# One layer of a pooling and short-conv decoder: the second norm of tiles 8-15 turned by DMA, conv and pooling work moved between engines, own buffers for the first tiles, a new order

## The reference, cut to what matters

```python
def trunk_layer(x, c, pool_buf, conv_buf, ffn_buf, pos0, ...):
    mod = (jax.nn.silu(c) @ w_ada + b_ada)[:, None, :]
    sh1, sc1, gt1, sh2, sc2, gt2 = jnp.split(mod, 6, axis=-1)
    h = rmsnorm(x, g_pre_mix) * (1 + sc1) + sh1
    proj = h @ w_in                                        # 1024 -> 2048
    v_pool, x_conv, gate_b, gate_c = jnp.split(proj, ...)  # 512 each
    y_pool = pool_mixer(...)     # window mean (2/4/8/16) - v, 128x128 map per group
    conv_in = jnp.concatenate([conv_buf, gate_c * x_conv], axis=1)
    y_conv = gate_b * causal_dwconv(conv_in, conv_w)       # 3 taps
    mix = jnp.concatenate([y_pool, y_conv], axis=-1) @ w_out
    x = x + gt1 * rmsnorm(mix, g_post_mix)
    h2 = rmsnorm(x, g_pre_ffn) * (1 + sc2) + sh2
    up = h2 @ ffn_w_up                                     # 1024 -> 5632
    a, b = jnp.split(causal_dwconv(ffn_in, ffn_conv_w), 2, axis=-1)   # ffn_in: carried rows, up
    f = (jax.nn.silu(a) * b) @ ffn_w_down                  # 2816 -> 1024
    x = x + gt2 * rmsnorm(f, g_post_ffn)
```

## Time and profile before

| | us |
|---|---|
| median of 3 runs (lowest, highest) | 727.0 (725.28, 727.85) |
| the profiled execution | 726.18 |
| its span on the slowest core (core 2) | 724.6 |
| spans of the 8 cores | 718.5 to 724.6 |
| TensorE busy | 694.0 (96%) |
| VectorE / ScalarE / GpSimd busy | 468.5 / 311.1 / 267.5 |
| granted TensorE clock, mean of core 2 | 0.989 |

### The profile page before, as it was taken

One profiled execution on the slowest core, in us unless ns is written; L12 is line 12 of the kernel. 1 busy time (PEld: TensorE's weight loads), 2 busy tenths in 40 slices (PEclk: granted clock), 3 DMA queues, 4 the chain that ended last, 5 costly groups with the idle time before them and its releaser, 6 DMA issues.

```text
span 724.6 us, 12059 instructions; the slowest of 8 cores (718.5 to 724.6 us)
## 1 busy us (share of the span) xinstructions
PE 694.0 (96%) x4049; PEld 331.3 (46%) x4049; DVE 468.5 (65%) x636; ACT 311.1 (43%) x554; POOL 267.5 (37%) x274
## 2 busy tenths in 40 slices
PE   5889989999989999999999999999999999999996
PEld 2445535444445544444444444444444444444442
DVE  2659699754659998777777411138777777758403
ACT  5255544334657764444544211144454544433111
POOL 1102255333858634424444132214333333223220
PEclk8999999999999999999999999999999999999999
DMA  8999877996999667556899964113335433061422
GB/s 249 161 240 181 194 124 131 156 192 169 178 277 275 221 116 124 97 127 100 147 156 155 221 222 137 58 59 59 59 66 95 74 59 59 1 228 68 144 105 72
DMA packets 23532, 100.71 MB, mean 139 GB/s; under 512 B 3184, under 2 KB 3696, under 8 KB 18608
## 3 DMA queue, kind: packets, MB, share of 16 engines
q0 software_dynamic: 9072, 47.71, 39.9%
q1 hardware_dynamic: 14400, 52.23, 22.6%
HBM read 127.02 MB, written 20.63 MB: 204 GB/s over the span
## 4 chain that ended last, share of the span: by engine, by line
PE 73%; DMA 14%; issue 4%; DVE 4%; POOL 2%; ACT 2%; DVEq 0%; SPq 0%; POOLq 0%; ACTq 0%
PE ps L520 72%; DMA big<-x 5%; DMA scp<-w_scp 3%; DMA y<-big 2%; POOL big L559 2%; DMA wsh<-w_sh 1%; DMA ring<-w_inc 1%; PE ps L530 1%; DVE big L555 1%; POOL by L559 1%; DVE ta L555 1%; DVE ss L559 0%; DVE q L555 0%; PE ps L538 0%; ACT xc L551 0%
## 5 line engine op out<-in xcount | busy, mean ns | idle before, releaser
L520 PE MATMUL ps<-ah,ring 128*128 128x512 bf16 (+2 forms) x2240 | 407.2, 342 | 4.4 <-DVE q L555 2.0
L520 PEld LDWEIGHTS ps<-ah,ring 128*128 128x128 bf16 x2240 | 187.8, 98 | 212.8 <-issue 6.6
L555 DVE SCALAR_TENSOR_TENSOR big<-ps,misc,big 128x1022 f32<-128x1022 f32 (+1 forms) x176 | 224.5, 1281 | 69.5 <-ACT halob L551 32.5
L559 POOL TENSOR_TENSOR g<-big 128x1024 bf16<-128x1024 f32 x44 | 104.5, 2375 | 171.6 <-DVE big L559 91.0
L551 ACT ACTIVATE big<-ps,misc 128x1024 f32<-128x1024 f32 x88 | 97.9, 1113 | 140.1 <-PE ps L520 139.9
L520 PE MATMUL ps<-wdn,g 128*128 128x512 bf16 x704 | 153.1, 379 | 0.0
L559 POOL TENSOR_TENSOR big<-big 128x256 f32<-128x256 f32 (+2 forms) x51 | 65.1, 1279 | 121.0 <-DVE big L555 94.1
L520 PEld LDWEIGHTS ps<-wdn,g 128*128 128x128 bf16 x704 | 68.5, 98 | 82.1 <-issue 0.4
L551 ACT ACTIVATE big<-ps 128x1024 bf16<-128x1024 f32 (+2 forms) x30 | 28.9, 964 | 123.4 <-PE ps L520 116.2
L666 DVE RECIPROCAL stat<-stat 128x1 f32<-128x1 f32 (+1 forms) x64 | 9.7, 157 | 106.3 <-ACT stat L551 105.6
L520 PE MATMUL ps<-wo,by 128*128 128x512 bf16 x256 | 58.2, 384 | 0.0
(11 more groups left out here) (130 smaller groups left out, 464.1 us busy)
## 6 DMA issues: line engine op xcount, KB each, us to landing
ring<-w_up POOLq DMA_DIRECT2D x22, 1024.0 KB, 9.9
y<-big SPq DMA_DIRECT2D x27, 512.0 KB, 3.2
big<-y SPq DMA_DIRECT2D x16, 512.0 KB, 3.8
big<-x SPq DMA_DIRECT2D x7, 1024.0 KB, 8.9
big<-x SPq DMA_DIRECT2D x12, 512.0 KB, 9.2
wdn<-w_down POOLq DMA_DIRECT2D x11, 512.0 KB, 12.8
wg<-w_gate POOLq DMA_DIRECT2D x4, 1024.0 KB, 11.1
scp<-w_scp POOLq DMA_DIRECT2D x8, 384.0 KB, 6.9
```

What stands on the lines that cost most here:

```text
L520: inst = e.matmul(bank_ap, l, r, start=(first and i == 0), stop=(last and i == len(pairs) - 1))
L555: return K.op(eng, lambda e: e.scalar_tensor_tensor(out, in0, s, in1, op0, op1), reads=reads, writes=writes, cost=c_dve(n))
L559: return K.op(eng, lambda e: e.tensor_tensor(out, in0, in1, op), reads=reads, writes=writes, cost=c_dve(n) if eng == "dve" else c_pool(n))
```

## The change

1. Second norm: tiles 0-15 are kept in eight buffers `xnp`. Tiles 0-7 are still turned by TensorE; tiles 8-15 by DMA transposes from `xnp` into `ah`, issued on SP during the first up projection (`turn_by_dma`), each followed per four tiles by the modulation. `xnp` lies over the modulation weights `w2` 0-3.
2. Third conv term: ScalarE scales it into `xc`, GpSimd adds it to `ta`; the product with b goes from GpSimd to VectorE.
3. Start: tiles 0-7 have seven `xn` buffers instead of three, and the squares are written to `junk` instead of `xn`. The square-root table of ScalarE is loaded before x arrives.
4. Smaller moves: the samples' window sums from VectorE to GpSimd, scaling of the pool map and the pool state's bias from VectorE to ScalarE; w_out waits for fewer regions.
5. A new `PROJ` order and three planner costs. `UPAT` is -1 three times, so the first `w_up` loads wait for the gate row as before.

```diff
 PROJ = """
-T:0 T:1 T:2 T:3 T:4 T:5 T:6 T:7 a:0 s:0,0 s:0,1 a:1 s:1,0 s:1,1 a:2 s:2,0 s:2,1 a:3 s:3,0 s:3,1 a:4 s:4,0 s:4,1
+T:0 T:4 T:1 a:0 T:2 T:3 T:6 a:1 a:2 s:0,0 T:7 T:5 s:1,0 s:0,1 s:2,0 s:1,1 a:3 s:3,0 s:2,1 s:3,1 a:4 a:5 a:6
...
+FIRST_T = 8
+UPAT = (-1, -1, -1)
...
-    RATE = 330e3
+    RATE = 315e3
...
+    XNP = [alloc("xnp", [128, D], BF16, at=cur[0] + 2048 * i) for i in range(8)]
...
+    XN += [alloc("xn", [128, D], BF16, at=cur[0] + 2048 * i) for i in range(4)]
...
+    JUNK = [alloc("junk", [128, D], BF16), alloc("junk", [128, D], BF16, at=ta_at)]
...
-        return (0.16 if mode > 1.0 or n < 256 else 0.21) + n / 960.0 / mode
+        return (0.19 if n < 256 else 0.16 if mode > 1.0 else 0.21) + n / 960.0 / mode
...
-        return 0.15 + n * 2.2 / 1000.0
+        return 0.15 + n * (2.2 if n < 512 else 2.7) / 1000.0
...
+    K.op("act", lambda e: e.activation(out=STAT[:, 7, 19:20], in_=EPSB, func=AF.Sqrt), reads=[r_sc, r_eps], cost=0.3)
...
+        if k == ST2 and t < 16:
+            N, r_n = XNP[t % 8], r_xnp[t % 8]
+        else:
+            j = t % (NXN + 4) if t < 8 else t % NXN
+            N, r_n = XN[j], r_xn[j]
...
+        if k == ST1:
+            h = t % 2 if t < 8 else 0
+            stats(X[0:rows, :], rows, k, t, [r_x], JUNK[h][0:rows, :], [r_junk[h]])
...
+    def turn_by_dma(t):
+
+        K.dma("sp", lambda e: [e.dma_start_transpose(out=AH[:, :, t * 128:t * 128 + 128], in_=XNP[t - 8])], s_xnp[t - 8], 1,
+              reads=[r_xnp[t - 8]], writes=[r_ah[kc][t] for kc in range(KC)], deps=[up_op[-1]], nbytes=524288, row=2048)
+        if t % 4 == 3:
+            modulate(list(range(t - 3, t + 1)), G2T, S2T, r_m2)
...
-            ts(POOLW[:, g, :], PWF[:, g, :], VECS[:, V_PSC + g:V_PSC + g + 1], None, ALU.mult, None, [r_pwf, r_vecs], [r_poolw], 128)
+            act(POOLW[:, g, :], PWF[:, g, :], AF.Copy, [r_pwf, r_vecs], [r_poolw], 128, scale=VECS[:, V_PSC + g:V_PSC + g + 1])
...
-                tt(dst[:, lo:W], src[:, lo:W], src[:, lo - sh:W - sh], ALU.add, [r_src], [r_dst], W - lo)
+                tt(dst[:, lo:W], src[:, lo:W], src[:, lo - sh:W - sh], ALU.add, [r_src], [r_dst], W - lo, eng="pool")
...
-        for m, w in ((1, w1), (0, w0)):
-            stt(sh(TA[k]), v[m], w, sh(TA[k]), ALU.mult, ALU.add, [rq, r_ta[k], r_vecs], [r_ta[k]], n)
+        act(sh(XC[k]), v[0], AF.Copy, [rq, r_vecs], [r_xc[k]], n, scale=w0)
+        tt(TA[k][:, 0:n], TA[k][:, 0:n], XC[k][:, 0:n], ALU.add, [r_ta[k], r_xc[k]], [r_ta[k]], n, eng="pool")
+        stt(sh(TA[k]), v[1], w1, sh(TA[k]), ALU.mult, ALU.add, [rq, r_ta[k], r_vecs], [r_ta[k]], n)
         if c < 4:
-            tt(BY[:, 4 + j, c0:c0 + n], TA[k], TB[k], ALU.mult, [r_ta[k], r_tb[k]], [r_by[4 + j][c]], n, eng="pool")
+            tt(BY[:, 4 + j, c0:c0 + n], TA[k], TB[k], ALU.mult, [r_ta[k], r_tb[k]], [r_by[4 + j][c]], n)
...
-                r.alias(pool_regs)
+                r.alias(r_v[0] + r_v[1] if hb == 0 else r_v[1][1:] + r_v[2] + r_v[3])
...
-            if t < 16:
+            if t < FIRST_T:
                 turn_tile(t, o_xn[t], "act" if t % 2 else "dve")
...
+            if gi == 0 and FIRST_T <= i + 6 < 16:
+                turn_by_dma(i + 6)
```

More of the change, by code:

```diff
@@ L677, in stats2 @@
              writes=[r_stat[k + 1][16]], cost=0.16)
-    r_xn = [R() for _ in range(NXN)]
-    xn_i = [0]
+    r_xn = [R() for _ in range(NXN + 4)]
+    r_junk = [R() for _ in range(2)]
     r_ah = [[R() for _ in range(17)] for _ in range(KC)]
@@ L697, in norm_tile @@
-        return j
-    def turn_tile(t, j, eng, bank=None):
+        if k == ST2 and t < 16:
[3 more added lines that the diff above has]
+            N, r_n = XN[j], r_xn[j]
+        if t == 16 and k == ST2:
+            stats2(X[:, 0:512], k, [r_x], N[:, 0:512], [r_n])
+            ts(N[:, 0:512], X[:, 0:512], STAT[:, k + 1, 16:17], None, ALU.mult, None, [r_x, r_stat[k + 1][t]],
+               [r_n], 512, mode=2.0)
+            return N, r_n
@@ new lines, in norm_tile @@
+        if k == ST1:
+            h = t % 2 if t < 8 else 0
+            stats(X[0:rows, :], rows, k, t, [r_x], JUNK[h][0:rows, :], [r_junk[h]])
+        else:
+            stats(X[0:rows, :], rows, k, t, [r_x], N[0:rows, :], [r_n])
+        ts(N[0:rows, :], X[0:rows, :], STAT[0:rows, k + 1, t:t + 1], None, ALU.mult, None,
+           [r_x, r_stat[k + 1][t]], [r_n], D, mode=2.0)
+        return N, r_n
+    r_xnp = [R() for _ in range(8)]
+    s_xnp = [new_sem("xnp%d" % i) for i in range(8)]
+    def turn_by_dma(t):
[3 more added lines that the diff above has]
+            modulate(list(range(t - 3, t + 1)), G2T, S2T, r_m2)
@@ L701, in turn_tile @@
+    def turn_tile(t, xn, eng, bank=None):
         r0, rows = tile_rows(t)
+        N, r_n = xn
         b = take() if bank is None else bank
         psb = PSF[:, b, :].bitcast(BF16).rearrange("p (k n) -> p k n", k=KC)
-        o = tr([psb[:, kc, 0:rows] for kc in range(KC)], [XN[j][0:rows, kc * 128:(kc + 1) * 128] for kc in range(KC)],
-           IDB[0:rows, 0:rows], [r_xn[j], r_idb], [r_bank[b]], 0.5)
+        o = tr([psb[:, kc, 0:rows] for kc in range(KC)], [N[0:rows, kc * 128:(kc + 1) * 128] for kc in range(KC)],
+           IDB[0:rows, 0:rows], [r_n, r_idb], [r_bank[b]], 0.5)
@@ L819, in tile_in @@
         turn_tile(t, p1a[t], TURNS[t], (turn_b + [None])[t % (5 - START)] if t < 8 else None)
+        if t == 7:
+            r_ta[0].alias(r_junk[1:])
+            for i in range(4):
+                r_s[i].alias(r_xn[NXN + i:NXN + i + 1])
     def start_step(kc, c):
@@ L1049, in ada2 @@
         if kc < 4:
-            r_usb.alias([r_w2[kc]])
+            for r in r_xnp:
+                r.alias([r_w2[kc]])
         elif kc < 6:
@@ L1186, in up_load @@
     def up_load(gi, pb):
-        up_slot[gi, pb] = ring_load(wup_d[pb], KC * 512, deps=gate_in if gi == 0 and pb < 3 else ())
+        up_slot[gi, pb] = ring_load(wup_d[pb], KC * 512, deps=() if gi or pb > 2 else [o_ops[UPAT[pb]]] if UPAT[pb] >= 0 else gate_in)
     r_yd = [R() for _ in range(17)]
@@ L1247, in o_mm @@
         for hb in range(2):
-            mm(PSF[0:rows, b + hb, :], [(BY[:, kc, r0:r0 + rows], WO[hb][:, kc, :]) for kc in range(KC)],
+            o_ops[t] = mm(PSF[0:rows, b + hb, :], [(BY[:, kc, r0:r0 + rows], WO[hb][:, kc, :]) for kc in range(KC)],
                [r_by[kc][c] for kc in range(KC)] + r_wo[hb], [r_bank[b + hb]], 512)
-    o_xn = {}
+    o_xn, o_ops = {}, {}
     singles[:] = [6, 7]
@@ L1348, in up_group @@
                     tmps[:] = [4, 5]
+            if gi == 0 and FIRST_T <= i + 6 < 16:
+                turn_by_dma(i + 6)
+            if gi == 0 and i == 10:
+                r_usb.alias(r_xnp)
             pb = i // 2
```

36 lines of the change are left out of this document (14 added, 22 removed).

## The result

The changed kernel takes 761.8 us (750.4 to 769.7, 4 runs) against 726.7 (725.3 to 727.9) for the kernel before in the same runs: ratio 1.041, interval 1.036 to 1.046. It is 4% slower; I had forecast 717.0.

A forecast was written before the change was run, and what follows sets the result against it. The prediction took TensorE's own work plus its losses before 300 us to bound the kernel. Gains of 3.6+0+2.9+3.5 = 10.0 us took the 727.0 us median to 717.0, range 712.5 to 724.5.

The forecast's parts named there:

- The DMA transposes: First up projection: eight 256 KB DMA transposes on SP, costed at nothing, covered by DMA room at share 0.65.
- Rival 1: Up projection: DMA transposes take the engines and TensorE waits; 734 us at 9.9 us each; chance 0.04.
- What stands behind them: Up projection: transposes' result first read by second up group, 16 modulations fit VectorE's slack; costed at nothing.
- Turns, 3.6 us: Output projection: eight fewer turns of tiles 8-15 on TensorE, 0.45 us each, 3.6 us gained.
- the other three terms: Start, projections' conv units and output projection's x stall: gains of 0, 2.9 and 3.5 us.
- Conv units, 2.9 us: Projections: work moved off VectorE recovers part of 7.5 us of TensorE idle and slow clock; 2.9 us gained.
- The x stall, 3.5 us: Output projection: earlier gate row and w_up loads shrink the wait for x; 3.5 us gained, bounds 0 and 4.7.
- Start, 0: Start: earlier gains are waited for again at 82.83 us; 0 us, ends 0.7 slower and 1 faster.
- The sum: Whole kernel: gains of 3.6, 0, 2.9 and 3.5 us make 10.0, for a median of 717.0 us.

The follow-up runs named there:

- plain_copy_in_up: Changed kernel with each DMA transpose replaced by a plain DMA copy of the same 256 KB, same places and queue; ratio to before 0.992.
- transposes_in_down: Changed kernel with all eight DMA transposes and their modulations moved to the first down projection; ratio to before 0.992, 0.991 when run again.
- before_and_down_turns: Kernel before with one part alone: tiles 8-15 kept in xnp and turned by DMA transposes during the first down projection; ratio 0.998.
- down_old_order_chain: transposes_in_down with both the order of steps and the conv chain of the kernel before; ratio to before 0.992.
- no_up_loads: Changed kernel with modulations held until later pairs and the w_up loads after the first three left out; ratio to before 0.994.
- modulate_late: Changed kernel with modulations of tiles 8-15 placed later in the code, at the nineteenth and twenty-first pair; ratio to before 1.052.
- modulate_held: Changed kernel with modulations of tiles 8-15 made to wait for matmuls of the eighteenth and twentieth pair; ratio to before 1.050, 766.3 us.

## Why the prediction was wrong

*The DMA transposes* are the step that failed: "I cost all of it at nothing; its cover is the DMA room". I bounded the price by a plain store, 2.1 us, and a w_up load, 9.9, and gave the outcome in which they take the engines 0.04. Alone a transpose takes 3.0 us, near the end that I took. But the price is not a property of the transfer: beside the weight loads it is 6 to 14 us on a lucky core of the changed kernel, up to 46 to 59 on the others, and the load's own goes from 9 to 45. Rival 1 had the right sign and the right place. It asked for an average of 7.8 us over all eight, and core 5 has 22.8; but it took this for a fixed price of one transfer, and what decided was the chance that a core collapses, 23 of 32 spans here, where one of eight is enough. Taken from plain_copy_in_up, which keeps all but the transposing (0.992 against 1.041), the step costs some 35 us. The cover that I named (share 0.65) was cover for bytes; and I counted the transposes' own bytes, not what they do to the packets of others.

*What stands behind them.* I said that the result is first read by the second up group, and put the 16 modulations on VectorE's slack. They stood in its in-order queue, and VectorE waited 19.3 us. That was an error too, but not the cause: held back, they save nothing.

*Turns, 3.6 us:* the mechanism was right, the size is not shown. Four of the eight lie behind the last w_out matmul, and from before to transposes_in_down that stretch goes from 160.5 to 158.7 us, 1.8 for four. But alone in the kernel before (before_and_down_turns) the same step gained 1.2 us in all (0.998), and the stretch grew to 161.8: TensorE sits idle there for 3.7 us on the mean of the cores, where before has 1.4, so new waits took what the turns gave. In the changed kernel the step is worth more than 3.6: 1.001 with the turns on TensorE, 0.992 with the eight in the down projection, on one chip, some 6 us. With the turns on TensorE the stretch is 165.4: TensorE waits for the second norm (up to 2.47 us before one turn; idle 4.5 us on the mean). What in the rest of the change brings these waits was not tried. So the other three terms, 6.4 us in my sum, gave nothing as long as TensorE did the turns (1.001).

*Conv units, 2.9 us:* wrong. The output projection does not start earlier, 172.9 us on the mean of the changed kernel and 173.9 and 174.7 in the two runs with the turns in the down projection, against 172.7; TensorE waits for q as before. Its idle time between 75 us and that start is 5.8 us on the mean of the cores and was 6.0; I had forecast 3 to 5. I moved 9.3 us off VectorE and took some of TensorE's 7.5 for it, without showing that those waits are VectorE's load and not the length of the chain from q, which the edit did not shorten.

*The x stall, 3.5 us:* the mechanism was right, gate row, w_up, y store and x in turn, with 1.7 us of wait left of 6.5 on core 2. The gate row's store is issued at 131.1 on core 5, where it was at 140.0 on core 2 of the kernel before, and takes 23.8 us where it took 26.5. The size was that of one core: core 2 and core 1 of the kernel before have the stall (65.4 and 66.3 us in the stage), cores 0 and 5 do not (60.3 and 61.0). The mean goes from 62.9 to 60.7 and 59.4; if the turns are 1.8 of it, 0.4 to 1.7 us are left for this term.

*Start, 0:* the second tile is turned at 82.7 as forecast, and the output projection starts no earlier. But before_and_down_turns (0.998) and down_old_order_chain (0.992) differ only in the start, the smaller moves, the buffers of the second norm and the planner's costs, 0.7% or 5 us, mostly in the output projection (60.8 to 59.0) and behind it (161.8 to 160.0). Which of them it is was not separated and stays open; so does how much of it is the chip.

*The sum:* with the transposing out of the way the kernel gains 5.7 us (721.35 against 727.09), not 10.0.

## What to carry to other kernels

Look at all cores before the page of the slowest: a cost that hits a core by chance is paid almost always when the time is the maximum of eight. Do not price a new kind of transfer from one of its size: ask what runs beside it, and try it at a quiet place first, since here a move of the same eight DMAs by some 130 us turned 4% slower into 0.8% faster. Try a part alone and also leave it out of the whole: the same turns were worth 1.2 us one way and some 6 the other. A term read from the slowest core's trace needs a look at the others: a stall that two or three of eight have is worth less than it shows.

## What the runs showed of the hardware

A DMA transpose of 128x1024 bf16 from SBUF to SBUF lands in 3.0 to 3.2 us alone, on eight cores at once, and its issue takes 1.22 us on SP (no_up_loads). Beside the 1 MB w_up loads, which cast to bf16 on GpSimd's queue, there are two outcomes. Either transposes and loads take up to some 16 us each (cores 1, 3 and 6 of the changed kernel: transposes up to 14.1, loads 8 to 17). Or both stall each other: transposes take up to 59.4 us and loads 38 to 47 on core 5, up to 71.7 for a transpose on core 4 of modulate_late, SP is held up to 36.4 us in one issue (modulate_held), and the DMA share is over 1 at 84 to 107 GB/s. Which of the two a core falls into changes from execution to execution. Where only one load at a time stood beside the transposes it did not happen: two w_gate loads, one at a time, beside three transposes (no_up_loads, 80 core spans), and one w_up load in the down projection (no span beyond 735 at a clock of 0.95 or more). Plain copies of the same bytes in the same 256-byte pieces at the same places never did it either (28 core spans). Whether the casting, the queue or the number of loads under way matters, and why the two kinds of packets stall each other, the runs do not tell.
